# Layer 0 of a two-layer streaming trunk: two of four trailing-pool groups move to GpSimd, the fourth channel tile's convolution moves ahead of the mixing, and one convolution round moves from TensorE to VectorE

## What is computed

```
z = h @ w_in
a = a_in[..., :512] * sigmoid(a_in[..., 512:])
a = causal_depthwise_conv(a, conv_w, conv_b)          # 31 taps, 512 channels
a = silu(layer_norm(a))
groups = [trailing_mean(p_in group i, window (2, 4, 8, 16)[i]) - p_in group i]   # 4 x 128 channels
p = einsum(groups, pool_w) * pool_scale
h = h + concatenate([a, p]) @ w_out
```

## Time and profile before

| | |
|---|---|
| median of 3 runs | 1080.72 us |
| the profiled execution | 1080.46 us |
| its span, first to last instruction | 1078.7 us |
| mean granted TensorE clock | 0.998 |
| TensorE busy | 1067.3 us |
| VectorE busy | 806.2 us |
| ScalarE busy | 530.6 us |
| GpSimd busy | 30.9 us |

### The profile page before, as it was taken

How to read it: one execution, slowest core, us unless ns; L and a number is a source line. 1 busy time by engine, 2 the same in 40 slices (tenths; PEclk the granted TensorE clock), 3 DMA queues, 4 the chain that set the end, 5 groups by cost and what they waited for, 6 DMA issues and landing times.

```text
span 1078.7 us, 19613 instructions
## 1 busy us (share of the span) xinstructions
PE 1067.3 (99%) x8190; PEld 992.5 (92%) x8190; DVE 806.2 (75%) x1161; ACT 530.6 (49%) x794; POOL 30.9 (3%) x85
## 2 busy tenths in 40 slices
PE   8999999999999999999999999999999999999997
PEld 8998999999999999999999877787898898898897
DVE  6899987876786786789563468757886896796785
ACT  7324454544454454467652256535544454454564
POOL 5050000000000000000000000000000000000000
PEclk9999999999999999999999999999999999999999
DMA  7361222234134125222232222222234135134121
GB/s 219 118 159 45 79 79 79 79 108 127 39 118 137 60 80 156 79 77 81 79 118 80 78 79 79 80 78 90 66 103 133 40 118 156 40 117 131 66 79 79
DMA packets 100469, 102.76 MB, mean 95 GB/s; under 512 B 3803, under 2 KB 96717, under 8 KB 100381
## 3 DMA queue, kind: packets, MB, share of 16 engines
q1 hardware_dynamic: 98780, 99.12, 29.5%
q0 software_dynamic: 1536, 2.32, 1.0%
q10 hardware_dynamic: 64, 0.07, 0.0%
HBM read 97.12 MB, written 2.10 MB: 92 GB/s over the span
## 4 chain that ended last, share of the span: by engine, by line
PE 95%; DVE 3%; ACT 1%; issue 0%; DMA 0%; DVEq 0%; ACTq 0%
PE ps L1872 56%; PE ps L2090 28%; PE ps L2161 4%; PE ps L2019 1%; PE ps L2122 1%; PE ps L1919 1%; PE ps L2254 1%; PE ps L2273 1%; PE ps L1880 1%; DVE w_lo L532 0%; ACT conv L775 0%; DMA xin<-in_x_dram 0%; PE ps L2149 0%; PE ps L2192 0%; DVE w_lo L571 0%
## 5 line engine op out<-in xcount | busy, mean ns | idle before, releaser
L1872 PE MATMUL ps<-u_lo,w_hi 128*128 128x264 f32 (+1 forms) x1120 | 299.5, 323 | 1.7 <-DVE u_lo L1299 1.7
L1872 PE MATMUL ps<-u_hi,w_hi 128*128 128x264 f32 (+1 forms) x1120 | 295.2, 320 | 0.0
L1872 PE MATMUL ps<-u_hi,w_lo 128*128 128x264 f32 (+1 forms) x1120 | 294.8, 319 | 0.0
L2090 PE MATMUL ps<-c_lo,w_hi 128*128 128x264 f32 (+1 forms) x868 | 245.9, 283 | 0.3 <-DVE w_lo L571 0.3
L2090 PE MATMUL ps<-c_hi,w_hi 128*128 128x264 f32 (+1 forms) x868 | 244.9, 282 | 0.0
L2090 PE MATMUL ps<-c_hi,w_lo 128*128 128x264 f32 (+1 forms) x868 | 244.7, 282 | 0.0
L525 ACT ACTIVATE w_hi<-raw 128x1024 fp32r<-128x1024 f32 x118 | 123.7, 1057 | 162.6 <-PE ps L1872 135.0
L1872 PEld LDWEIGHTS ps<-u_lo,w_hi 128*128 128x128 f32 x1120 | 184.8, 188 | 20.2 <-issue 4.8
L1872 PEld LDWEIGHTS ps<-u_hi,w_hi 128*128 128x128 f32 x1120 | 185.9, 188 | 16.5 <-issue 1.2
L1872 PEld LDWEIGHTS ps<-u_hi,w_lo 128*128 128x128 f32 x1120 | 185.5, 188 | 15.4
L532 DVE TENSOR_TENSOR w_lo<-raw,w_hi 128x1024 fp32r<-128x1024 f32 x118 | 143.7, 1223 | 64.8 <-ACT w_hi L525 63.1
(11 more groups left out here) (266 smaller groups left out, 1306.5 us busy)
## 6 DMA issues: line engine op xcount, KB each, us to landing
raw<-in_ffn_w_dram SPq DMA_DIRECT2D x64, 1024.0 KB, 5.5
raw<-in_gla_w_in_dram SPq DMA_DIRECT2D x12, 1024.0 KB, 5.4
raw<-in_cp_w_in_dram SPq DMA_DIRECT2D x8, 512.0 KB, 5.4
raw<-in_cp_w_out_dram SPq DMA_DIRECT2D x4, 1024.0 KB, 5.2
raw<-in_gla_w_out_dram SPq DMA_DIRECT2D x4, 1024.0 KB, 5.1
shifted<-conv_in POOLq DMA_DIRECT2D x32, 69.5 KB, 2.1
xin<-in_x_dram SPq DMA_DIRECT2D x4, 512.0 KB, 5.5
raw<-in_cp_w_in_dram SPq DMA_DIRECT2D x2, 1024.0 KB, 5.0
```

The costliest lines, as they stand in the source:

```text
L1872: last = mm(ps[:, n % NS, c:c + b - a], l, r[:, a - origin:b - origin], start=(k == 0 and i == 0), stop=(k == count - 1 and i == 2))
L2090: last = mm(bank, l[:, 0, j, :], r, start=(fresh and j == 0 and m == 0), stop=(j == KD // 2 - 1 and m == 2), skip_group_check=not fresh)
```

## The change

- TensorE does 6 rounds for tile 2 where it did 7; VectorE does the 4 taps (7 in place of 3 for this tile).
- `conv_taps(3)` comes directly behind p3; the four `mix` follow it. ScalarE evacuates the convolution of tile 3 ahead of `mix_hi(0)`.
- Groups 0 and 1 (windows 2 and 4) are built on GpSimd, behind its DMA issues for tile 3. The mean minus self is one scaling, one short product and one subtraction there, each waiting for the one before where it needs its result.
- On VectorE `run_taps(20, (0, 1))` stands ahead of the two `split_lo` of `B_OUTP`, then all taps left of tiles 0, 1 and 2 in one run, then groups 2 and 3. Group 2 waits for `pd_ready` 2. No tap is left to stand between the additions.
- On ScalarE both `split_hi` of `B_OUTP` come behind the copy of `pin` 0 and ahead of that of `pin` 1. The high parts of groups 0 and 1 stand between the copies of `pin` 2 and `pin` 3.

```diff
-PE_ROUNDS = {2: ROUNDS - 1, 3: ROUNDS - 1}
+PE_ROUNDS = {2: ROUNDS - 2, 3: ROUNDS - 1}
-CONV_STEP, POOL_STEP = 11, (0, 5, 1, 0)
+CONV_STEP, POOL_STEP = 20, (0, 0, 3 * TAPS, 0)
+POOL_GROUPS = 2
-    order += [("mix", 0), ("mix", 1), ("conv", 3), ("mix", 2), ("mix", 3)]
+    order += [("conv", 3), ("mix", 0), ("mix", 1), ("mix", 2), ("mix", 3)]
...
+            pool.wait_ge(pin_zeroed, 1)
+            done = 0
+            for g in range(POOL_GROUPS):
+                evacuated(pool, SLOT["p", g])
+                src = p_in = pin[:, g, :]
+                for j in range(g + 1):
+                    back = 1 << j
+                    pool.tensor_tensor(win[:, j % 2, WMAX:], src[:, WMAX:], src[:, WMAX - back:-back],
+                                       ALU.add).then_inc(pool_step, 1)
+                    done += 1
+                    pool.wait_ge(pool_step, done)
+                    src = win[:, j % 2, :]
+                short, pd = (2 << g) - 1, work[g]
+                pool.tensor_scalar(pd[:, short:], src[:, WMAX + short:], 1.0 / (short + 1), None,
+                                   ALU.mult).then_inc(pool_step, 1)
+                pool.tensor_tensor(pd[:, 0:short], src[:, WMAX:WMAX + short], rcount[:, 0:short],
+                                   ALU.mult).then_inc(pool_step, 1)
+                done += 2
+                pool.wait_ge(pool_step, done)
+                pool.tensor_tensor(pd[:, :], pd[:, :], p_in[:, WMAX:], ALU.subtract).then_inc(pd_ready, 1)
...
@@ scalar
                 act.activation(pin[:, g, WMAX:], slot_ap(n), ACT.Copy).then_inc(evac[n % NS], 1)
-                if g % 2:
-                    if g == 1:
-                        split_hi(2 * B_OUTP)
-                        split_hi(2 * B_OUTP + 1)
-                    for i in (g - 1, g):
+                if g == 0:
+                    split_hi(2 * B_OUTP)
+                    split_hi(2 * B_OUTP + 1)
+                if g >= POOL_GROUPS:
+                    for i in (2 * g - 4, 2 * g - 3):
                         act.wait_ge(pd_ready, i + 1)
                         act.activation(a_hi[:, i, :], work[i], ACT.Copy).then_inc(pd_hi_ready, 1)
...
-                if g == 2:
+                if g == 0:
                     evac_conv(3)
                 mix_hi(g)
...
@@ vector
             run_taps(CONV_STEP, (0, 1))
             dve.wait_ge(pin_zeroed, 1)
-            for g in range(PG):
+            split_lo(2 * B_OUTP)
+            split_lo(2 * B_OUTP + 1)
+            for g in range(POOL_GROUPS, PG):
                 n = SLOT["p", g]
                 run_taps(POOL_STEP[g], (0, 1, 2))
                 evacuated(dve, n)
+                if g == POOL_GROUPS:
+                    dve.wait_ge(pd_ready, POOL_GROUPS)
...
-                if g % 2:
-                    if g == 1:
-                        split_lo(2 * B_OUTP)
-                        split_lo(2 * B_OUTP + 1)
-                    for i in (g - 1, g):
+                if g >= POOL_GROUPS:
+                    for i in (2 * g - 4, 2 * g - 3):
                         dve.wait_ge(pd_hi_ready, i + 1)
...
@@ tensor
-            mix(0)
-            mix(1)
             conv_taps(3)
-            mix(2)
-            mix(3)
+            for g in range(PG):
+                mix(g)
```

More of the change, by code:

```diff
@@ L381, in build_trunk @@
         dve_step = sem("dve_step")
+        pool_step = sem("pool_step")
         pin_zeroed = sem("pin_zeroed")
```

## The result

The changed kernel takes 1088.57 us (median of 4 runs, 1087.30 to 1089.59) against 1080.76 of the kernel before; the ratio is 1.0073, with a 95% interval of 1.0061 to 1.0085. It is slower, by 7.8 us where 9.3 were forecast.

The account below looks back on a forecast made before the run. TensorE was taken as the bound, VectorE as the second. 1080.46 us plus 2.2 for the later mean plus 7.1 lost by VectorE to GpSimd gave 1089.8, range 1082 to 1093.

Parts of the forecast that it names:

- TensorE, the round: Second convolution on TensorE: the removed round is worth 0.91 us, so conv 3 starts at 94.90.
- the signs: Listed trace evidence, including stretched VectorE taps, TensorE waits at mix 2 and outp 0 of about 10 us, conv 2 at 5.5.
- VectorE's list, +2.8 and 2.2 on the mean: VectorE up to group 3: changed taps and additions add 2.8 us, making the mean 2.2 us late without any clash.
- ScalarE: Both high weight parts precede pin 1's copy, now at 86.0 instead of 84.9; GpSimd's group 1 cannot start earlier.
- GpSimd's own length: Groups 0 and 1 on GpSimd: instructions sum to 8.4 us, done alone at about 92, covered by 4.5 us.
- What GpSimd costs VectorE, 7.1 us: Ahead of group 3, GpSimd and VectorE take turns; nine instructions hold VectorE up by 7.1 us; chance 0.52.
- some 0.14 us of start was hidden: Each of nine held GpSimd instructions hides 0.14 us of start, so VectorE loses 8.4 - 9 x 0.14 = 7.1 us.
- Only GpSimd waits: Rival: GpSimd waits for VectorE's taps, which never wait; 1082.7 us, chance 0.28.
- Kept out: Rival: GpSimd cannot work while taps run and works with VectorE idle from 96.5; 1092.5 us, chance 0.15.
- In time: Rival: VectorE is in time at mix 2, so only the 0.91 us round counts; 1079.6 us, chance 0.05.

Follow-up runs that it names:

- GpSimd only wrote: The changed kernel with GpSimd's nine instructions for groups 0 and 1 replaced by one memset per group, values left out: 1082.69 us, ratio 1.0025.
- taps alternated: The changed kernel with VectorE's run of 20 taps drawn from tiles 0, 1 and 2: 1088.27 us, ratio 1.0073.
- GpSimd worked for nobody: The kernel before, VectorE's list untouched, GpSimd doing the same nine kinds of instruction into a spare tile nobody reads: 1085.81 us, ratio 1.0054.

## Why the prediction was right

- **TensorE, the round.** Right: conv 2 took 5.55 where it took 6.44, and conv 3 started within 0.02 us of the forecast. As forecast, the gain was lost in waits, but not where the signs put them (mix 2 and outp 0, together about 10 us). The profiled execution has 3.85 at mix 0, 2.13 at mix 2 and 0.27 at outp 0: the low part of group 0 stands behind group 2 in VectorE's list, so what delays group 2 is waited for at mix 0 already.
- **VectorE's list, +2.8 and 2.2 on the mean.** Right, and shown by itself where GpSimd only wrote: group 2 at 96.54 and group 3 at 104.78 are the forecast's 96.5 and 104.8, and the time lay 2.4 above the kernel before.
- **ScalarE.** Right: pin 1 was copied behind both splits (85.32 to 85.91), GpSimd's second group began at 86.81 behind the first, so this cost nothing.
- **GpSimd's own length**, 8.4 us: 9.3 alone. Additions were taken too long (1.24 for 1.07), subtractions a little too short (1.24 for 1.33), scalings much too short (0.89 for 1.55). The Trainium skill's GPSIMD Engine Reference, section Elementwise, came to 1.14 by estimate for two inputs; additions at 1.07 and subtractions at 1.33 lie around it.
- **What GpSimd costs VectorE, 7.1 us.** The mechanism was right, the size off: 4.7 measured. The failing step is "some 0.14 us of start was hidden": it took VectorE to stand for nearly all of each instruction. Measured in the trace of the changed kernel, three additions cost 0.69 each, two subtractions 0.96 and 1.06, two scalings 0.24 and 0.42 (the second of them held a split, not a tap), the short ones nothing: 4.75. Why so much and no more isn't known; with GpSimd's true length of 9.3 the same step would have given 8.0. Taking 4.7 for 7.1 puts the sum at 1087.4; the profiled execution took 1087.3.
- **A term that the sum lacks: TensorE's clock.** It fell in the new waits, which cost the profiled execution nothing and a second trace of the same kernel 1.4 us (last section). The right prices give 6.9 us, and that the median came out at 7.8, nearer to the 9.3, is luck: the price that was too high stood in for a term that was left out.
- **Rivals.** "Only GpSimd waits" (1082.7) fell with the stretched taps. "Kept out" did not happen in the changed kernel, where the addition issued at 79.87 got in at the first dependent tap (81.54), but it did for 8 us where taps alternated. "In time" fell with the waits at mix 0 and mix 2.

The Trainium skill (SBUF — State Buffer, sections SBUF: two separate sides and Who interferes with whom) has the one that starts second blocked for the whole instruction of the other. The trace agrees that both directions block, and that a write alone does not. It differs in the length: the tap at 83.04 ended at 84.05, while the scaling that had held it up went on to 84.42, and an addition of 1.07 cost 0.69; only the tap of 2.14, where GpSimd worked for nobody, lost more than the addition lasted. It also differs in who goes first: where taps alternated, an addition that began at 80.07 let the eight taps and two splits behind it pass until 88.5. Here the measurements decide.

## What to carry to other kernels

An instruction on GpSimd that reads tiles was not free here beside a VectorE that reads two: price it in VectorE's time. In the changed kernel and with the additions doubled, an addition lent to GpSimd cost VectorE 0.69 to 0.8 us, when VectorE does it in 0.62 itself. And work taken from the bounding engine must not go to the engine that it next waits for: look where that one's list is due before adding to it, and at the PSUM slots that its additions free before moving anything within it.

## What the runs showed of the hardware beyond that

TensorE's granted clock fell behind the wait of 3.85 us, as the stretches of the changed kernel show (busy time and count of PE, PEld, DVE, ACT, POOL; then PEclk, DMA share, GB/s):

```profile
102.00:105.00 3.00, 0.00 (x0) 0.00 (x0) 2.90 (x7) 0.52 (x1) 0.00 (x0) 1.00 0.00 0
...
106.00:107.00 1.00, 1.00 (x6) 1.00 (x6) 0.96 (x2) 0.00 (x0) 0.00 (x0) 0.50 0.00 0
...
110.00:111.00 1.00, 0.69 (x6) 0.72 (x6) 0.87 (x2) 1.00 (x3) 0.00 (x0) 1.00 0.00 0
```

At 0.50, the lower level of 1.2 GHz, mixes 0 and 1 took about 2.8 us (105.21 to 107.98) where they took 1.55. In this execution it cost nothing, since mix 2 had to wait until 110.31 anyway, and by then the clock was back at 1.00.

The trace of the changed kernel timed again (1088.64 us) has VectorE's group 3 done at 109.46, as here, and the same start of mix 2, 110.31. But there the clock was still at 0.50 when mix 2, mix 3 and the first part of outp 0 ran:

```profile
113.00:114.00 1.00, 1.00 (x7) 1.00 (x6) 0.55 (x1) 0.67 (x2) 0.00 (x0) 0.50 0.00 0
115.00:116.00 1.00, 1.00 (x10) 1.00 (x9) 0.96 (x2) 0.93 (x1) 0.00 (x0) 1.00 0.00 0
```

The mean starts at 122.58 in place of 121.19, 1.39 later, and the time is 1.34 longer. Over the whole execution the granted clock was 0.997 in the first trace and 0.994 in the second. It was 0.994 or 0.996 in the other seven executions of the changed kernel, which took 1087.5 to 1089.6 us; that they lost time in the same place isn't shown, since they have no trace.
